# Six adaLN units moved from ahead of the prompt's QKV product into the heads stage

## The reference

```python
m = jax.nn.silu(cvec) @ w + b                    # adaLN: 1024 -> 6 * 1024, for c and for c_ctx
sh1, sc1, g1, sh2, sc2, g2 = jnp.split(m, 6, axis=-1)
h = rms_norm(x, norm_mix) * (1 + sc1) + sh1
q, k, v = qkv_heads(h, wqkv, qn, kn)             # q, k normalised per head; latents also rotated
p = softmax([q k^T * 64**-0.5, sink])            # latent queries: own keys and 128 cached keys
x = x + g1 * (p v @ wo)
x = x + g2 * moe(rms_norm(x, norm_ffn) * (1 + sc2) + sh2)
```

## Time and profile before

| | us |
|---|---|
| median of 3 runs | 1283.17 (1282.88 to 1284.16) |
| the profiled execution, its own time | 1284.74 |
| its span, first to last instruction | 1282.9 |
| PE busy | 1255.7 (98%) |
| DVE busy | 444.4 (35%) |
| ACT busy | 328.3 (26%) |
| mean granted TensorE clock | 0.996 of 2.4 GHz |
| DMA moved | 497.44 MB, mean 388 GB/s |

### The profile page before, as it was taken

How to read it: one execution, slowest core, us unless ns; L and a number is a source line. 1 busy time by engine, 2 the same in 40 slices (tenths; PEclk the granted TensorE clock), 3 DMA queues, 4 the chain that set the end, 5 groups by cost and what they waited for, 6 DMA issues and landing times.

```text
span 1282.9 us, 18946 instructions
## 1 busy us (share of the span) xinstructions
PE 1255.7 (98%) x6950; PEld 695.9 (54%) x6950; DVE 444.4 (35%) x1508; ACT 328.3 (26%) x736; POOL 72.5 (6%) x119
## 2 busy tenths in 40 slices
PE   7999999999999999999999899999999999999998
PEld 5776775544454445444454477554455445544544
DVE  3596272222222222222235727322222222222223
ACT  2486331221122112211122523222122211221211
POOL 0395000000000000000010020000000000000000
PEclk8999999999999999999999999999999999999999
DMA  9988999999999999999997787899999999999994
GB/s 328 383 329 360 406 417 383 415 420 419 421 420 420 421 421 420 420 420 420 419 407 322 167 366 263 288 404 418 419 420 420 420 420 421 420 421 421 419 419 193
DMA packets 90760, 497.44 MB, mean 388 GB/s; under 512 B 11273, under 2 KB 20145, under 8 KB 38480
## 3 DMA queue, kind: packets, MB, share of 16 engines
q1 hardware_dynamic: 90128, 496.48, 96.1%
q10 hardware_dynamic: 576, 0.22, 0.1%
HBM read 493.26 MB, written 3.41 MB: 387 GB/s over the span
## 4 chain that ended last, share of the span: by engine, by line
PE 93%; DVE 3%; ACT 2%; DMA 1%; issue 1%; ACTq 0%; POOL 0%; DVEq 0%
PE ps L1105 35%; PE ps L1139 18%; PE ps L1150 10%; PE ps L1076 7%; PE ps L781 4%; PE ps L706 4%; PE ps L834 3%; PE ps L1012 2%; PE ps L659 2%; PE ps L1125 1%; PE ps L1060 1%; PE ps L1117 1%; DMA W<-in_norm_ffn_dram 1%; PE ps L719 1%; PE ps L679 1%
## 5 line engine op out<-in xcount | busy, mean ns | idle before, releaser
L1105 PE MATMUL ps<-ring,xg 128*64 128x512 f32 x1344 | 296.4, 593 | 0.3
L1105 PEld LDWEIGHTS ps<-ring,xg 128*64 128x64 f32 x1344 | 101.5, 137 | 189.6 <-issue 175.2
L1105 PE MATMUL ps<-S,xg 128*64 128x512 f32 x704 | 154.8, 592 | 0.0
L1139 PE MATMUL ps<-ring,W 128*64 128x512 f32 x672 | 153.5, 598 | 0.0
L2186 DVE TENSOR_TENSOR ypart<-ps,ypart 128x512 fp32r<-128x512 f32 x128 | 88.5, 691 | 179.7 <-ACT ypart L1641 179.7
L2175 DVE SCALAR_TENSOR_TENSOR vec<-silu_h,W,ps 128x256 f32<-128x256 f32 x64 | 30.7, 480 | 332.2 <-ACT silu_h L1635 332.2
L1150 PEld LDWEIGHTS ps<-comb,ypart 128*128 128x128 f32 x1024 | 126.5, 191 | 18.6 <-issue 18.6
L1150 PE MATMUL ps<-comb,ypart 128*128 128x256 f32 x1024 | 135.3, 285 | 0.0
L1635 ACT ACTIVATE silu_h<-ps 128x256 f32<-128x256 f32 x64 | 24.7, 385 | 406.6 <-PE ps L1105 406.6
L1630 ACT ACTIVATE xg<-ps 128x384 f32<-128x384 f32 x176 | 83.3, 492 | 167.9 <-PE ps L1076 167.9
L1641 ACT ACTIVATE ypart<-ps 128x512 fp32r<-128x512 f32 x128 | 76.5, 597 | 184.6 <-PE ps L1139 184.6
(11 more groups left out here) (288 smaller groups left out, 1101.7 us busy)
## 6 DMA issues: line engine op xcount, KB each, us to landing
ring<-in_exp_w_down_dram SPq DMA_DIRECT2D x86, 1024.0 KB, 17.5
ring<-in_exp_w_gate_dram SPq DMA_DIRECT2D x78, 1024.0 KB, 15.9
ring<-in_exp_w_up_dram SPq DMA_DIRECT2D x78, 1024.0 KB, 18.3
S<-in_exp_w_down_dram SPq DMA_DIRECT2D x44, 1024.0 KB, 17.6
S<-in_exp_w_gate_dram SPq DMA_DIRECT2D x40, 1024.0 KB, 17.4
S<-in_exp_w_up_dram SPq DMA_DIRECT2D x40, 1024.0 KB, 19.0
ring<-in_ada_w_dram SPq DMA_DIRECT2D x24, 1024.0 KB, 20.3
S<-in_ada_w_dram SPq DMA_DIRECT2D x16, 1024.0 KB, 15.2
```

Source lines behind the costliest of these rows:

```text
L1105: mm = pe.matmul(PGU[64 * b:64 * b + 64, :].rearrange("p (h f) -> p h f", h=2), xg[:, places[k][m], 64 * b:64 * b + 64], gate_up_of(w[b])[ ...
L1139: mm = pe.matmul(bank[64 * b:64 * b + 64, :], hidT[:, j, 64 * b:64 * b + 64], down_of(w[b])[:, j, n * 512:(n + 1) * 512], start=(j == 0), ...
```

## The change

- Units 2 to 7 no longer stand ahead of `qkv_product(0, 0)`. There row 4 is closed after units 0 and 1 (`stop` at unit 1) and goes its way (copy, transposes, bias) as a partial sum.
- Units 2 to 7 are multiplied within the heads stage and added up in bank 7 as a second partial sum (`start` at unit 2). ACT copies it to a new place, `row_rest`, after `output_copy(2)` and ahead of `exps(7)`; PE turns it after T7; DVE adds it to what is in `mod` (`rest=True`). `mod_ready` counts one more from there on.
- Units 8 to 15 move to later places among the heads and are added up in bank 1.
- So that bank 1 is free, the prompt's scores of four heads now fill one bank (`scored`): banks 0 and 2. `maxima` takes one reduction over 4 x 128 in place of two over 2 x 128.
- SP issues units 9 and 10 where it issued units 9 to 15, and units 11 to 15 behind the four parts of `wo`.

```diff
+        row_rest = ring_f[:, 2 * EW + 3072:2 * EW + 3584]
...
+        def scored(g, b, q):
+
+            if g == 0:
+                return ps[2 * b][:, q * T:(q + 1) * T]
+            return ps[2 * b + q // 2][:, (q % 2) * 2 * T:(q % 2 + 1) * 2 * T]
...
-                    load_ada(range(EARLY + 9, N_UNITS))
+                    load_ada(range(EARLY + 9, EARLY + 11))
                     sp.wait_ge(at_qkv, 7)
                     for j in range(NKV):
                         b = j % 2
                         sp.dma_start(wo[HD * b:HD * b + HD, QG * (j // 2):QG * (j // 2 + 1), :],
                                      attn_wo[0, QG * HD * j:QG * HD * (j + 1), :].rearrange("(q d) n -> d q n", d=HD)
                                      ).then_inc(ld_wo, 16)
+                    load_ada(range(EARLY + 11, N_UNITS))
...
-                                       start=(k == 0), stop=(k == KC - 1))
+                                       start=(k == 0 or u == EARLY + 2), stop=(k == KC - 1 or u == EARLY + 1))
...
-            def ada_transposes(e, bank):
-                pe.wait_ge(ada_rows, e + 1)
+            def ada_transposes(n, row, bank):
+                pe.wait_ge(ada_rows, n)
...
-                    ada_products(range(EARLY + 2, EARLY + 8), ps[2])
                     qkv_product(0, 0)
-                    ada_transposes(4, ps[2])
+                    ada_transposes(5, ada_row(4), ps[2])
...
-                                mm = pe.matmul(ps[2 * b + q // 2][:, (q % 2) * 256:(q % 2) * 256 + keys],
+                                mm = pe.matmul(scored(g, b, q),
...
-                    ada_products([EARLY + 8], ps[7])
-
+                    ada_products([EARLY + 2], ps[7])
                     at_transposes(0)
-                    ada_products([EARLY + 9], ps[7])
+                    ada_products([EARLY + 3], ps[7])
                     at_scores(1)
                     at_transposes(1)
-                    ada_products([EARLY + 10], ps[7])
+                    ada_products([EARLY + 4], ps[7])
                     at_values(0)
 
+                    ada_products([EARLY + 5], ps[7])
                     at_transposes(2)
+                    ada_products([EARLY + 6], ps[7])
                     at_scores(2)
-                    ada_products([EARLY + 11], ps[7])
+                    ada_products([EARLY + 7], ps[7])
                     at_transposes(3)
+                    ada_products([EARLY + 8], ps[1])
                     at_values(1)
 
+                    ada_products([EARLY + 9], ps[1])
                     at_transposes(4)
-                    ada_products([EARLY + 12], ps[7])
+                    ada_products([EARLY + 10], ps[1])
                     at_scores(3)
                     at_transposes(5)
-                    ada_products([EARLY + 13], ps[7])
+                    ada_products([EARLY + 11, EARLY + 12], ps[1])
                     at_values(2)
 
-                    ada_products([EARLY + 14], ps[7])
+                    ada_products([EARLY + 13], ps[1])
                     at_transposes(6)
-                    ada_products([EARLY + 15], ps[7])
+                    ada_products([EARLY + 14], ps[1])
                     at_transposes(7)
+                    ada_transposes(6, row_rest, ps[7])
+                    ada_products([EARLY + 15], ps[1])
                     at_values(3)
-                    ada_transposes(5, ps[7])
+                    ada_transposes(7, ada_row(5), ps[1])
                     project(wo, oT, at_otc, 4, ld_wo, AB, 3, NKV)
...
-            def ada_copy(e, bank):
-                act.wait_ge(ada_used, KC * (e + 1))
-                act.activation(ada_row(e), bank[:, :], ACT.Copy).then_inc(ada_rows, 1)
+            def ada_copy(units, row, bank):
+                act.wait_ge(ada_used, units)
+                act.activation(row, bank[:, :], ACT.Copy).then_inc(ada_rows, 1)
...
-                    ada_copy(4, ps[2])
+                    ada_copy(EARLY + 2, ada_row(4), ps[2])
...
-                            ada_copy(5, ps[7])
+                            ada_copy(N_UNITS, ada_row(5), ps[1])
                         output_copy(m)
+                        if m == 2:
+                            ada_copy(EARLY + 8, row_rest, ps[7])
...
-                    ins = dve.tensor_tensor(
-                        mod[:, l, cd, 16 * b:16 * b + 16].rearrange("p (j q) -> p j q", j=4), src,
-                        adab[:, l, 2 * b:2 * b + 2, :].rearrange("p s (j q) -> p (s j) q", j=2), ALU.add)
+                    out = mod[:, l, cd, 16 * b:16 * b + 16].rearrange("p (j q) -> p j q", j=4)
+                    bias = adab[:, l, 2 * b:2 * b + 2, :].rearrange("p s (j q) -> p (s j) q", j=2)
+                    ins = dve.tensor_tensor(out, src, out if rest else bias, ALU.add)
...
-                        for b in range(2):
+                        for b in range(1 + g):
+                            n = QG // (1 + g)
                             ins = dve.tensor_reduce(
-                                mx[:, 2 * b:2 * b + 2],
-                                ps[2 * (i % 2) + b][:, :].rearrange("p (h s) -> p h s", h=2)[:, :, 0:keys],
-                                AX_X, ALU.max)
+                                mx[:, n * b:n * b + n],
+                                ps[2 * (i % 2) + b][:, :].rearrange("p (h s) -> p h s", h=n), AX_X, ALU.max)
...
-                    ada_finish(5, ps[7])
-                    dve.wait_ge(mod_ready, 6)
+                    ada_finish(4, ps[7], rest=True)
+                    ada_finish(5, ps[1])
+                    dve.wait_ge(mod_ready, 7)
```

More of the change, by code:

```diff
@@ L666, in keep_clock @@
                     pe.matmul(bank[:, 0:P], ones, ident, start=True, stop=True)
-            def ada_transposes(e, bank):
-                pe.wait_ge(ada_rows, e + 1)
+            def ada_transposes(n, row, bank):
+                pe.wait_ge(ada_rows, n)
                 for q in range(4):
-                    mm = pe.transpose(bank[:, q * P:(q + 1) * P], ada_row(e)[:, q * P:(q + 1) * P], ident)
+                    mm = pe.transpose(bank[:, q * P:(q + 1) * P], row[:, q * P:(q + 1) * P], ident)
                 mm.then_inc(ada_cols, 1)
@@ L818, in _ @@
                     sum_squares(2, 7, 0, 6)
-                    ada_transposes(1, ps[1])
+                    ada_transposes(2, ada_row(1), ps[1])
                     keep_clock(ps[5], 4)
@@ L823, in _ @@
                     project(w2, dwo, cn_ready, 1, ld_w2, CB)
-                    ada_transposes(2, ps[2])
+                    ada_transposes(3, ada_row(2), ps[2])
                     ada_products(range(3 * KC, 3 * KC + 4), ps[0])
@@ L1028, in _ @@
                 if l == 0:
-                    ada_transposes(3, ps[6])
+                    ada_transposes(4, ada_row(3), ps[6])
                     shared_hidden(1).then_inc(sh_gate, 1)
@@ L1376, in affine @@
                 else:
-                    act.wait_ge(mod_ready, 3 * l + (1 if which == 0 else 3))
+                    act.wait_ge(mod_ready, 4 * l + (1 if which == 0 else 3) - l * (which == 0))
                 for k in range(KC):
                     if l == which == 0 and k == 4:
-                        ada_copy(0, ps[2])
+                        ada_copy(1 * KC, ada_row(0), ps[2])
                         act.wait_ge(mod_ready, 1)
@@ L1483, in _ @@
                     conv_squares(6, 7)
-                    ada_copy(1, ps[1])
+                    ada_copy(2 * KC, ada_row(1), ps[1])
                     conv_squares(7, KC)
@@ L1493, in _ @@
                                        ).then_inc(cn_ready, 1)
-                    ada_copy(2, ps[2])
+                    ada_copy(3 * KC, ada_row(2), ps[2])
                     for k in range(KC):
@@ L1559, in exps @@
                             ins = act.activation(prob[:, i % 2, q, 0:keys],
-                                                 ps[2 * (i % 2) + q // 2][:, (q % 2) * 256:(q % 2) * 256 + keys],
+                                                 scored(g, i % 2, q),
                                                  ACT.Exp, bias=stat[:, m:m + 1], scale=HD ** -0.5,
@@ L1603, in _ @@
                     affine(l, 1)
-                    ada_copy(3, ps[0])
+                    ada_copy(4 * KC, ada_row(3), ps[0])
                     act.wait_ge(rt_logits, l + 1)
@@ L1717, in _ @@
                 pool.tensor_tensor(sq[:, 0, 0:T], sq[:, 0, 0:T], sq[:, k, 0:T], ALU.add).then_inc(y_added, 1)
-            pool.wait_ge(mod_ready, 6)
+            pool.wait_ge(mod_ready, 7)
             for g in range(G):
@@ L1747, in _, with ada_finish @@
             dve.memset(upad[:, :, :, PAD + T:], 0.0)
-            def ada_finish(e, bank):
+            def ada_finish(e, bank, rest=False):
                 l, b = divmod(e, 3)
-                dve.wait_ge(ada_cols, e + 1)
+                dve.wait_ge(ada_cols, e + 1 + (rest or e == 5))
                 for cd in range(2):
```

(17 more changed lines are left out.)

2 lines of the change are left out of this document (1 added, 1 removed).

## The result

| | before | after |
|---|---|---|
| median, us | 1283.57 (22 runs) | 1285.95 (22 runs) |
| ratio | | 1.0017, 95% interval 1.0011 to 1.0023 |
| profiled execution, its own time / span | 1284.74 / 1282.9 | 1285.91 / 1284.1 |

The change costs 2.2 us, with an interval of 1.4 to 3.0. The ratio leaves out one disturbed execution of each kernel (1615.48 and 1314.04 us).

What follows compares the result with a forecast made beforehand. PE, busy 98% of the span, was taken as the bound. 5.29 us taken out and 2.1 put in gave -3.2; late landings made it +1.5, the clock +2.0: 1285.2 us, range 1282.2 to 1287.6.

Steps and rivals of the forecast that it cites:

- What is taken out: Ahead of the prompt's QKV product: removing units 2 to 7 makes the heads stage start 5.29 us earlier.
- What is put in: Heads stage, all units landed: moved PE work and ACT's extra copy make project 2.1 us late.
- ACT's copy ahead of exps(7): Heads stage: copying the second partial sum adds 0.5 us on ACT before exps(7), the scaling and T7.
- unit 15 behind T7: Heads stage: unit 15 takes 1.0 us ahead of V3, whose 0.79 of idle hides part.
- The landings: Units 11 to 15 queue behind wo; unit 11 lands at 734.5, PE waits 2.5 us, project starts 1.5 us later than before.
- wo's rate: wo's four parts in SP's queue: 207 GB/s with the DMA engines fully busy, so 20.3 us for 4.19 MB.
- The clock: In PE's waits for late units: a fall likelier than none, 3.4 us at half speed, making +1.5 into +1.9 or +2.6.
- The sum: Whole kernel: -3.2 us if units have landed, +1.5 with the landings, +2.0 taken with the clock.
- After project: From project through the experts' stage: same order, PE sets the pace, nothing added or given back.
- the units land in time: Rival, heads stage: loads pass wo or wo is faster at its earlier place; -3.2 us, 1280.0, chance 0.14.
- Waiting costs more: Rival, heads stage: clock falls late or twice, or landings at the upper bound; +2.6 to +4.5 us, chance 0.28.

Runs made afterwards that it cites:

- e1: The changed kernel with units 11 to 15 not loaded, against the changed kernel; S0 to project 40.6 us, total not comparable.
- e6: e5 with unit 15 directly behind unit 14 and ACT's second partial-sum copy behind exps(7); 1278.89 us, ratio 0.9966 to the kernel before.
- e10: The changed kernel run again unaltered, for another profile; 1285.56 us, ratio 1.0013 to the kernel before, S0 to project 45.0 us.
- e7: The changed kernel plus 9 small matmuls ahead of unit 11 and 6 between units 11 and 12; 1284.45 us, ratio 1.0006 to the kernel before.
- e2: The changed kernel with wo loaded over 128 partitions, its rows on other partitions than the product reads; S0 to project 40.6 us, total not comparable.
- e4: The changed kernel with wo's two upper-partition parts issued from POOL's queue, the lower two from SP's; 1281.74 us, ratio 0.9983 to the kernel before.
- e5: The changed kernel with wo over 128 partitions in its right rows and V's product writing both halves; 1279.61 us, ratio 0.9970 to the kernel before.

## Why the prediction was right

- **What is taken out**: 5.3 us predicted, 5.5 in the profiles (46.4 and 40.9 us from the first QKV product to S0). No other wait appeared ahead of S0.
- **What is put in**: 2.1 predicted, 2.0 in e1, place by place. e6 takes two of its terms back, ACT's copy ahead of exps(7) and unit 15 behind T7, and gains 1.0 of the 2.0.
- **The landings**: unit 11 was to start 734.5 - 701.65 = 32.85 us after S0. It started 32.8 after (the change's profile) and 32.5 (e10, e7), with the others 2.5 us apart. The step that carried the forecast, to take expert 0's gate load as the stand-in for unit 11, held within 0.4 us. Without the clock, project was to start 45.35 us after S0, and did after 45.0.
- **wo's rate**: 207 GB/s, 210 after, 412 to 418 in e2. So the same bytes move at twice the rate once they are spread over 128 partitions. The prediction weighed two pages of the Trainium skill. The 341 GB/s of the Trainium skill's DMA: Bandwidth & Descriptors, section Bandwidth, stand there under transfers over 128 partitions, which the prediction did not say, so they never spoke of these loads. The Trainium skill's SBUF — State Buffer, section on the DMA port swizzle, says that 64 partitions reach half the ports. The halved rate agrees with it; the ports themselves no trace shows. The same page of the Trainium skill, section "Can I just issue two DMAs to hit both halves?", says that two transfers to different halves serialise and gain only 6%. From one queue the trace agrees (207 and 210 GB/s, the parts alternating between the halves); from two queues e4 measured 283, 37% more than 207.
- **The clock**: right in kind, mis-sized, and it is no certainty. The term was a fall of 3.4 us for +0.4 to +1.1, from 735.4 or later, that is, 33.75 us after S0. It fell 32.6 us after S0, still within the first wait, for 6.8 us, and cost 1.5; in e10 it didn't fall at all. Whether a fall is "likelier than none", as the forecast had it, the runs don't settle (e10).
- **The sum**: -5.5 + 2.0 + 4.4 = +0.9 us without a fall and +2.4 with one, against +1.5 and +1.9 to +2.6. The measured 2.2 us (1.4 to 3.0) lies between. That it comes so close to the forecast's 2.0 is in part luck: the terms without the clock came out 0.6 us too high, and the price of a fall too low by 0.4 or more.
- **After project** nothing was added or given back: from project's start to the end of the span it is 537.4 us before, after and in e10.
- **The rivals**: "the units land in time" was ruled out by its own sign, PE's wait on an adaLN load. As a kernel it exists: it is e5. "Waiting costs more" (+2.6 or more) is not ruled out for every execution: the one profiled with a fall comes to +2.4, next to its border.

## What to carry to other kernels

Filling an engine's idle time with moved work is sound only if the moved work's data, and that of the work it displaces, can still be there; ask which buffers come free later, and behind what the reloads now stand. A transfer that was hidden can hold back others for its whole length, so read its rate, not only its slack: here 4 MB on 64 partitions at a time took twice the DMA time of 4 MB on 128, which cost nothing in the kernel before and 4.4 us in the one after. A full share of busy DMA engines doesn't tell the two apart (1.04 at 207 GB/s, 1.02 at 418). Change the order only after having shown that the queue's total fits; if it doesn't, every order has a loser.

## What the runs showed of the hardware that was not expected

- Whether the clock falls in a given wait differs between executions of one kernel: the same waits (2.4 and 2.05 us, then 0.6 and 1.4) came once with 6.8 us at 1.2 GHz and once with none, worth 1.5 us in the stage. At layer 1's start the kernel before fell in its profile (654.8 to 658.3), the changed one did not, with the same work ahead. One such fall was worth 1.1 us, so the profile of one execution can be a us off another's by this alone.
- Two DMA queues that fill the lower and the upper 64 partitions side by side moved 283 GB/s together (e4, 713 to 720), above one half's 207 and far below 420.
- A product of 512 columns onto 64 rows can be cut into two of 256 onto both halves at no cost (1.08 us for V2 either way).
